# Two transformer blocks on one core: fp32r products in the expert loop, norms and pooling by pairs, modulation in one bank

## The reference

```
first_block, for l in 0, 1:
    h = rms_norm(x);  q, k, v, u, cq, ckv, kpe, gates = split(h @ w_in[l])
    y_a = swa_attention(...)      # window of 128, 8 heads, bias by bucket
    y_b = conformer_conv(u)       # 31 taps, layer norm, silu
    y_c = mla_attention(...)      # 8 heads, dense causal
    x += sum(sigmoid(gates) * ([y_a, y_b, y_c] @ w_branch[l])) @ w_out[l]
    x += square(relu(rms_norm(x) @ w_up[l])) @ w_down[l]
x = rms_norm(x)

second_block, for i in 0, 1:      # ALPHA = 4 ** 0.25
    m = split(silu(c) @ w_mod[i] + b_mod[i], 6)           # 6 x 1024
    y = mixer_retention_na(x * (1 + m[1]) + m[0], ...) if i == 0 else pool_mixer(same)
    x = layer_norm(ALPHA * x + m[2] * y, g, b)
    y = hier_moe(x * (1 + m[4]) + m[3])
    x = layer_norm(ALPHA * x + m[5] * y, g, b)

pool_mixer(h), for group g of 256 features, w = 2, 4, 8, 16:
    z = mean of h over tokens [t - w/2, t + w/2) (clipped to 0..256)  -  h
    out = (z @ pool_w[g]) * pool_scale

hier_moe(t): group = argmax over 4, in it the top 2 of 8 experts, weights by softmax
    acc += (silu(t @ wg) * (t @ wu)) @ wd * weight        # 32 experts, hidden 512
```

## Time and profile before

| | us |
|---|---|
| three runs | 2491.52, 2491.7, 2495.52; median 2491.7 |
| the profiled execution, its own time | 2489.5 |
| its span in the profile | 2487.7 |
| PE busy | 2302.5 (93%) |
| DVE busy | 1003.0 (40%) |
| ACT busy | 457.0 (18%) |
| DMA | 621 MB, 250 GB/s over the span |
| the chain that ended last | PE 85%, DVE 12%, issue 1%, ACT 1%, DMA 1% |

### The profile page before, as it was taken

One profiled execution on the slowest core, in us unless ns is written; L12 is line 12 of the kernel. 1 busy time (PEld: TensorE's weight loads), 2 busy tenths in 40 slices (PEclk: granted clock), 3 DMA queues, 4 the chain that ended last, 5 costly groups with the idle time before them and its releaser, 6 DMA issues.

```text
span 2487.7 us, 31019 instructions
## 1 busy us (share of the span) xinstructions
PE 2302.5 (93%) x12984; PEld 1596.9 (64%) x12984; DVE 1003.0 (40%) x2100; ACT 457.0 (18%) x729; POOL 3.8 (0%) x12
## 2 busy tenths in 40 slices
PE   7998989998999989998997899999995699999996
PEld 6876779997876679997976544444433444444443
DVE  7888535541266335546375311111106511111112
ACT  2112114330123214334242100000000000000000
POOL 0000000000000000000000000000000000000000
PEclk9998999999999999999998899999997899999998
DMA  6435643444435724442213599999974199999991
GB/s 246 165 136 203 248 158 136 169 169 145 160 139 217 288 102 160 178 164 100 99 71 157 213 420 427 427 427 427 428 325 203 60 411 425 425 430 427 426 427 58
DMA packets 43340, 621.45 MB, mean 250 GB/s; under 512 B 4816, under 2 KB 4816, under 8 KB 5232
## 3 DMA queue, kind: packets, MB, share of 16 engines
q1 hardware_dynamic: 33984, 489.93, 48.9%
q10 hardware_dynamic: 8640, 125.83, 11.9%
q0 software_dynamic: 624, 4.39, 0.4%
HBM read 619.08 MB, written 1.05 MB: 249 GB/s over the span
## 4 chain that ended last, share of the span: by engine, by line
PE 85%; DVE 12%; issue 1%; ACT 1%; DMA 1%; DVEq 0%; SPq 0%; ACTq 0%
PE bank L525 24%; PE bank L1087 18%; PE bank L1109 9%; PE sums L1117 5%; PE bank L708 3%; PE bank L709 3%; PE bank L710 3%; PE sums L710 2%; PE sums L709 2%; PE sums L708 2%; DVE wide L1631 2%; PE bank L546 2%; DVE arena L1658 2%; PE bank L535 2%; PE bank L836 2%; PE bank L838 2%
## 5 line engine op out<-in xcount | busy, mean ns | idle before, releaser
L525 PE MATMUL bank<-h,ring 128*128 128x256 f32 x1600 | 359.6, 386 | 15.1 <-DVE h L1556 12.1
L525 PEld LDWEIGHTS bank<-h,ring 128*128 128x128 f32 x1600 | 307.0, 193 | 65.7 <-DVE h L1556 12.9
L1109 PE MATMUL bank<-ring,wide 128*64 128x512 f32 x1024 | 233.8, 598 | 0.0
L1858 DVE TENSOR_TENSOR ring_split<-ring,arena_split 128x2048 fp32r<-128x2048 f32 x64 | 143.8, 2288 | 110.6 <-ACT arena_split L1322 110.4
L2255 DVE TENSOR_TENSOR wide<-bank,wide 128x256 f32<-128x256 f32 x64 | 27.2, 425 | 394.7 <-ACT wide L1485 394.7
L2260 DVE COPY wide<-bank 128x512 f32<-128x512 f32 x64 | 44.3, 692 | 345.1 <-PE bank L1109 345.1
L1485 ACT ACTIVATE wide<-bank 128x256 f32<-128x256 f32 x64 | 24.5, 383 | 751.2 <-PE bank L1087 751.2
L708 PE MATMUL bank<-h_split,arena_split 128*128 128x256 f32 x512 | 146.6, 286 | 15.0 <-DVE ring_split L1858 15.0
L1109 PEld LDWEIGHTS bank<-ring,wide 128*64 128x64 f32 x1024 | 67.8, 136 | 130.8 <-issue 130.8
L525 PE MATMUL bank<-arena,ring 128*128 128x256 f32 x496 | 118.4, 401 | 31.3 <-DVE arena L2301 19.7
L709 PE MATMUL bank<-scratch_split,arena_split 128*128 128x256 f32 x512 | 146.2, 285 | 0.0
(11 more groups left out here) (314 smaller groups left out, 3429.4 us busy)
## 6 DMA issues: line engine op xcount, KB each, us to landing
ring<-in_stream SPq DMA_DIRECT2D x100, 2048.0 KB, 7.8
ring<-in_experts SPq DMA_DIRECT2D x98, 2048.0 KB, 10.0
arena<-in_experts SPq DMA_DIRECT2D x34, 2048.0 KB, 15.2
ring<-in_experts ACTq DMA_DIRECT2D x30, 2048.0 KB, 13.4
arena<-in_experts ACTq DMA_DIRECT2D x30, 2048.0 KB, 13.3
wide<-in_na_bias POOLq DMA_DIRECT2D x1, 1536.0 KB, 9.6
arena<-in_consts POOLq DMA_DIRECT2D x1, 1088.0 KB, 6.4
x<-in_tokens SPq DMA_DIRECT2D x1, 1024.0 KB, 6.0
```

Source lines behind the costliest of these rows:

```text
L525: mm = pe.matmul(dst, a, b, start=(first and i == 0), stop=(i == len(terms) - 1))
L1109: mm = pe.matmul(banks[2][64 * half:64 * half + 64, :], M["turned"][:, e % 2, at:at + 64], w[:, k, 512 * half:512 * half + 512], start=(k ...
L1858: dve.tensor_tensor(split["ring"][:, slot, 2048 * part:2048 * part + 2048], v, HI[("up", "down")[part]][:, j % 2, :].bitcast(F32), ALU.sub ...
```

## The change

Six things at once.

1. **Modulation in one bank a layer.** All 12 chunks of a layer add up in sums[0]. Chunk c takes `cond` shifted by 2c columns, so that its two rows stand at rows 2c and 2c + 1 of each group of 32. One copy on ACT, one turn (`turn_mod`, 4 products of 24 columns) behind the out-projection and one add on DVE follow, in place of 12 of each.
2. **Attended values in sums[1] and sums[3].** `open_attended` uses these two in turn, and not the rotating banks.
3. **fp32r in gather and spread.** Rows of tokens are split in a high part (fp32r, written by ACT) and a low part (`rows_low`, by DVE, difference of bank and high part); the 0/1 matrices are fp32r. A gather is 8 fp32r products in place of 4 of fp32. y is scaled by its slot's weight and split in the same way, the high part by ACT (it waits `down_done` and the weight), the low part by DVE; the turned `weighted` becomes 0/1 by a compare on DVE, and the slot's weight is the sum over its row, by ACT's `accum_out`. A spread is 16 fp32r products of 64 rows in place of 8 of fp32. Gate, up and down stay as they were. The copy of what was turned is cut from 512 to 256 columns.
4. **Norms by pairs of tiles.** Each of the four pairs has its own event, for the residual (`added`), centring (`centred`), squares (now on ACT), scaling by the root (`scaled_by_root`) and h (`h_act`, and `h_dve` for the last pair). Gain, shift and modulation are folded into columns worked out early (`norm_columns`). ACT writes h for tiles 0 to 5 and all of x, DVE h for tiles 6 and 7. The router runs pair by pair, and the output is stored in four DMAs.
5. **Band pooling on PE.** `pool_rows(g)` multiplies h by the pooling weights with tokens on the rows, DVE copies the bank, `pool_band_of(g)` multiplies it by a 256 x 256 band matrix of group g (1 MB in all, loaded by POOL). DVE's box sums go.
6. The prologue's and the loop's memsets of fp32r buffers are products with 0.

```diff
             def mod_site(l, c):
...
+                at = cond_at - 2 * c
+                for k in range(KT):
+                    g = 32 * (k % 4)
+                    mm = pe.matmul(sums[0][g:g + 32, :], cond[:, k, at:at + 32], w[:, k, :], start=(c == 0 and k < 4),
+                                   stop=(c == MOD_CHUNKS - 1 and k >= 4), skip_group_check=True)
+                S.give(mm, "mod_product", l, c)
...
-                if c:
-                    S.wait(pe, "mod_copied", l, c - 1)
-                    if c >= 2:
-                        S.wait(pe, "mod_kept", l, c - 2)
-                    for t in range(4):
-                        mm = pe.matmul(sums[2][:, 2 * t:2 * t + 2], A["mod_rows"][:, (c - 1) % 2, t * P:(t + 1) * P], cst("sum4"),
-                                       start=True, stop=True)
...
+            def open_attended(l, pair):
+
+                b = 1 + 2 * (pair % 2)
+                if pair >= 2:
+                    S.wait(pe, "read", "y", l, pair - 2)
...
                     for a in range(2):
                         k = 2 * j + a
+                        c = (k % 4) * P
                         mm = product(bank[:, a * T:(a + 1) * T],
-                                     [(M["by_token"][:, t, k * P:(k + 1) * P], placed_at[buf][:, t, :]) for t in range(2)])
+                                     [(MS["by_token"][:, t, k * P:(k + 1) * P], place_split[buf][:, t, :]) for t in range(2)]
+                                     + [(rows_low[:, 2 * t + k // 4, c:c + P], place_split[buf][:, t, :]) for t in range(2)])
...
+                    for m in range(4):
+                        for part in (MS["y"], M2S["y_low"]):
+                            for n in (m, m + 4):
+                                a, c = 64 * (n // 4), m * P
+                                pe.matmul(sums[n // 2][:, (n % 2) * T:(n % 2 + 1) * T], part[a:a + 64, c:c + P],
+                                          MS["turned"][a:a + 64, before, T:2 * T], start=False, stop=False, skip_group_check=True)
...
-                        act.activation(M["turned"][:, e % 2, :], banks[1][:, :], ACT.Copy)\
+                        act.activation(M["turned"][:, e % 2, 0:T], banks[1][:, 0:T], ACT.Copy)\
                            .then_inc(S.sem(f"moe{i}_turned"), 1)
+                        act.activation(smax[:, 1, T:2 * T], banks[1][:, T:2 * T], ACT.Copy,
+                                       accum_out=slot_weight[:, e % 2:e % 2 + 1]).then_inc(S.sem(f"moe{i}_weight_summed"), 1)
+                        act.wait_ge(S.sem(f"moe{i}_down_done"), it * 4 + (e + 1))
+                        act.wait_ge(S.sem(f"moe{i}_weight_summed"), it * 4 + (e + 1))
+                        act.activation(MS["y"], banks[2][:, :], ACT.Copy, scale=slot_weight[:, e % 2:e % 2 + 1])\
+                           .then_inc(S.sem(f"moe{i}_y_high"), 1)
...
-                        dve.wait_ge(S.sem(f"moe{i}_down_done"), it * 4 + (e + 1))
-                        dve.tensor_copy(M["y"], banks[2][:, :]).then_inc(S.sem(f"moe{i}_y_kept"), 1)
...
+                        dve.wait_ge(S.sem(f"moe{i}_weight_summed"), it * 4 + (e + 1))
+                        dve.tensor_scalar(MS["turned"][:, e % 2, T:2 * T], banks[1][:, T:2 * T], 0.0, None, ALU.is_gt)\
+                           .then_inc(S.sem(f"moe{i}_slots_turned"), 1)
+                        dve.wait_ge(S.sem(f"moe{i}_y_high"), it * 4 + (e + 1))
+                        dve.scalar_tensor_tensor(out=M2S["y_low"], in0=banks[2][:, :], scalar=slot_weight[:, e % 2:e % 2 + 1],
+                                                 in1=MS["y"].bitcast(F32), op0=ALU.mult, op1=ALU.subtract)\
+                           .then_inc(S.sem(f"moe{i}_y_kept"), 1)
...
+                for b in range(4):
+                    act.wait_ge(S.sem("centred"), S.value("centred", i, s, b))
+                    S.give(act.activation(pair_of(scratch, b), pair_of(x, b), ACT.Square), "post_squares", i, s, b)
+                root(("post", i, s))
...
+                for b in range(3):
+                    act.wait_ge(S.sem("scaled_by_root"), S.value("scaled_by_root", i, s, b))
+                    for k in (2 * b, 2 * b + 1):
...
+                            ins = act.activation(h[:, k, :], x[:, k, :], ACT.Identity, scale=norm_col(i, s, "h_gain", k),
+                                                 bias=norm_col(i, s, "h_shift", k))
+                    S.give(ins, "h_act", i, s, b)
...
+            pe.wait_ge(S.sem("band_landed"), 16)
+            pool_rows(0)
+            pool_rows(1)
+            pool_band_of(0)
+            pool_rows(2)
+            pool_band_of(1)
+            pool_rows(3)
+            pool_band_of(2)
+            pool_band_of(3)
```

More of the change, by code:

```diff
@@ L285, in two_blocks_kernel @@
         scratch = whole["scratch"]
-        wide = sb("wide", [P, 8192])
+        wide = whole["wide"]
         arena = whole["arena"]
@@ L2094, in post_norm @@
                 tag = ("post", i, s)
-                centre(tag, x, KT, D, ("sum", *tag))
+                twice = [P, 2, T]
+                bank = take(dve, "sum", *tag)
+                mean = bank[:, 0:T].unsqueeze(1).to_broadcast(twice)
+                for b in range(4):
+                    v = x[:, 2 * b:2 * b + 2, :]
+                    n = S.give(dve.scalar_tensor_tensor(out=v, in0=mean, scalar=-1.0 / D, in1=v, op0=ALU.mult, op1=ALU.add),
+                               "centred", i, s, b)
@@ L2206, in route @@
                 link(ins)
+                for t, half in ((0, 1), (1, 0), (1, 1)):
+                    keep_low(t, half)
                 bank = take(dve, "rank", i)
```

296 lines of the change are left out of this document (170 added, 126 removed).

## The result

The changed kernel took 2382.5 us (median of four runs, 2380.0 to 2388.1) where the kernel before took 2491.6: a ratio of 0.956, interval 0.954 to 0.958. The prediction was 2385, the range 2358 to 2420. The profiled execution took 2380.0 us with a span of 2378.1, 109.6 less than the 2487.7 of before; the sum of the prediction was 106.6.

The account below looks back on a forecast made before the run. Expert loops were taken as bound by PE and loads at once, layers mostly by PE, seams by DVE and PE alternating. 27 + 20 + 9.2 - 2.6 + 42.8 + 10.2 = 106.6 us off 2489.5, plus 2.2, gave 2385; range 2358 to 2420.

Parts of the forecast that it names:

- Layers: First two layers: modulation in one bank and attended values in their own banks save 27 us, bounds 13 and 34.
- the two DVE waits: Layer 0: DVE's waits of 5.60 and 3.18 us at modulation adds go, together 8.8 us.
- PE's wait with its half-rate stretch: Layer 0: PE's 5.43 us wait for ScalarE's copy of attended values and the half-rate stretch behind go, 5.3 us.
- Loops: Two expert loops: loads become the only bound, each loop ends 9.9 us earlier; 20 us, bounds 8 and 32.
- Entry: Loop entries: faster first gathers save 9.2 us in all, DVE's low parts of rows cost 2.6.
- Norms: Norms, router and output store: work by pairs of tiles saves 42.8 us, bounds 30 and 48.
- Pooling: Band pooling on PE: 25.5 us for 35.7, including a new 2.4 us wait; saves 10.2, bounds 5 and 15.
- A: Rival: expert loops give nothing back, queues alternate and DMA share falls below 1; 2405 us, chance 0.12.
- B: Rival: layers give nothing, DVE or the softmax chain takes up what PE leaves; 2412 us, chance 0.15.
- E: Rival: the load stream speeds up with PE, loops save 103 us instead of 20; 2302 us, chance 0.03.
- C: Rival: seams give more, full clock and no pool wait, 74 us for 59.6; 2370 us, chance 0.12.
- D: Rival: PE pauses in every loop turn, clock falls to half, gain about cancelled or kernel slower; chance 0.03.

Follow-up runs that it names:

- no_spread: Changed kernel without the spread's 16 products an expert inside the loop, all experts but each loop's last missing from the result: 2381.1 us.
- half_loads: Changed kernel with each expert load, except a loop's first six, cut from 2 MB to 1 MB, half of each weight stale: 2308.1 us.
- u_att_mod: Changed kernel with attended values back in the rotating banks and modulation again chunk by chunk: 2412.9 us.
- all_sp: Changed kernel with SP issuing all of an expert's loads, including the middle third that ScalarE issued: 2375.8 us.
- u_loop: Changed kernel with gather and spread back in fp32, one copy of rows and y, no low parts: 2407.0 us.
- u_pairs: Changed kernel with each wait of the four norms for a pair of tiles made a wait for the last pair: 2430.8 us.
- pool_banks: Changed kernel with band products of the third and fourth pooled group in two accumulators of their own, sums 1 and 3: 2378.8 us.
- warm: Changed kernel with unread products added where PE waits, after three norms' sums of squares and ahead of each loop's entry gather: 2377.6 us.

## Why the prediction was right, and where its steps were off

**What bounds the kernel.** Right, and tested in both directions: a shorter turn leaves the loop where it is (no_spread), shorter loads make it 425 us at once (half_loads).

**Layers, 27 predicted, 30.8 measured.** In layer 0 (17.1 for 17) the scores of the last unit come at 248.5 for 263.4, 14.9 us earlier, where the two DVE waits (8.8) and PE's wait with its half-rate stretch (5.3) made 14.1; the rest gave 2.2 for 2.9. The terms are as predicted, not only their sum. That it fits to 0.1 us is luck: three other profiled executions of the same layer ended it 5 us later. Layer 1 is the mis-sized one, 13.8 for 10. PE's waits there for ScalarE's copy of attended values, before and after (us in total, times, longest):

```profile
PE bank L525 <- ACT arena L1186: 3.4, 7, 0.5
```

```profile
PE bank L549 <- ACT arena L1258: 0.8, 1, 0.8
```

There were seven such waits, and I had counted the four on the part of the chain that I had read. The split can be read by setting the starts of the same PE instruction in the two traces against each other, row by row. The lead of the changed kernel grows at each of the eleven sites, not at nine only, by 0.91 us each, the distance from a site's start to the next row's in the kernel before:

```profile
750.68 1.05 PE L777 MATMUL sums<-con,arena 128*128 128x2 f32 x8
751.59 0.53 PE L546 MATMUL bank<-con,smax 128*128 128x128 f32 x3
```

That makes 10.0 for 8.8. The waits for ScalarE's copy give 2.9 for 1.7. A stretch at half clock, which the kernel before had at this place and the changed one did not, gives 1.6 that the sum did not have (windows of the kernel before and, at the same work, the changed one):

```profile
730.00:733.00 3.00, 3.00 (x18) 0.59 (x16) 2.08 (x9) 0.97 (x4) 0.00 (x0) 0.51 0.00 0
712.00:715.00 3.00, 3.00 (x26) 1.35 (x25) 2.76 (x11) 1.29 (x5) 0.00 (x0) 1.00 0.00 0
```

Elsewhere in the layer 0.7 went to the clock, and 13.8 is the sum. The clock's part is of these two executions and no gain to count on: in u_att_mod a further stretch of half clock made layer 1 3.8 us longer than before. The bounds 13 and 34 held.

**Loops, 20 predicted, 18.6 measured.** The landing times were right: the last load lands 447.3 us behind the first product in both loops (449.2 predicted). Window around it in the second loop:

```profile
2335.00:2340.00 5.00, 5.00 (x26) 1.62 (x24) 0.75 (x1) 0.69 (x1) 0.00 (x0) 1.00 0.64 265
```

The fp32r products were a little slower than their nearest rows: gather 1.06 for 0.96, spread 1.14 for 0.96 (0.12 apart, but the first of each block later), a turn 13.2 for 12.9. The other end of the bound, halves that don't overlap, is out. What I had wrong is the pause: not 1.8 us in each turn but 2.49 in every second or third, because two queues carry the loads. all_sp shows it: one queue, one pause of 1.24 a turn. The two loops end 13.6 and 16.2 us behind the last landing, where the sum had 12.5. Most of the difference between them is the clock. In the second loop the last of these pauses stands ahead of the last expert but one, whose gate and up then ran partly at half clock:

```profile
2323.30 8.79 PE L1136 MATMUL bank<-ring,h 128*64 128x512 f32 x32 [2.49 <-DMA ring<-in_experts]
...
2338.24 7.04 PE L1136 MATMUL bank<-arena,h 128*64 128x512 f32 x32
```

That expert took 14.94 us, the one at this place in the first loop 13.24, 1.7 of the 2.6 us by which the two loops differ.

**Entry, 6.6 predicted, 7.5 measured.** The gather gave 4.0 and 4.6 for 4.6 each, the low parts took 0.1 and 1.0 for 1.3 each. u_loop gives back 6.0 of it.

**Norms, 42.8 predicted.** Closing products to centring fell by 4.0 (4.4 predicted), centring to variance is 5.16 (5.3), and the router starts 1.96 us behind the scaling's start (1.9). The last norm with the store gave 11.3 for 12.6: centring and variance gave 4.0 and 4.9 for 4.4 and 4.7, so scaling and store gave 2.4 for 3.5. u_pairs adds what the prediction did not have: how much clock the pairs save, 10.6 us. I had put the pairs down as hidden work alone; where I let the clock fall, at the router, it fell (7.01 us as predicted).

**Pooling, 10.2 predicted.** From the scaling to the next centring 23.7 us for the 25.5 of the working, a gain of 12.0. The wait that was forecast at 2.4 is there with 2.34, and pool_banks takes it away. The half rate was over-sized: the first two groups took 5.1 us where 7.0 had been put.

**The rivals.** A (the loops give nothing) falls by the 18.6 us of u_loop, B (the layers give nothing) by the 30 of u_att_mod, E (the stream speeds up) by no_spread. C was right in its first half only: the seams gave 60.2 for 59.6 and not 74, and the pool wait was there; warm shows that a full clock at the seams has to be paid for with work. D came in part: after 11 of the 18 longer pauses gate and up ran below full clock (8.78 mostly), 1.7 us each, and the 14.68 of the loads hid it but for the last one of the second loop. Had PE been the bound, all of it would have been seen in the time. So one sign that I had named for being wrong, the clock's rows falling inside the loop, did come; the time is right because the loads, and not PE, are the bound there.

The Trainium skill (TensorE: Matmul & The Clock Gate, "Loop structure matters more than you think") had warned of that shape. The trace agrees for pauses of 2.49 us in part of the turns; at 1.83 in every turn (no_spread, 1500 to 1600) and at 1.24 (all_sp) the clock stood at 1.00. The Trainium skill's other place that was weighed (DMA: Bandwidth & Descriptors, "Where 436 GB/s comes from") puts the ceiling at 435 GB/s; the loops stayed at 427 to 429 in the changed kernel, no_spread and all_sp, and ended no 8 us earlier on that account.

## What to carry to other kernels

When a loop stands at two limits at once, work taken from one of them is paid only at the loop's ends; ask how far the last load's landing and the last product are apart, and whether the loads land in the order in which they are used. At a seam between stages, handing over by pairs of tiles was worth more than the sum of the steps that it overlaps, since PE's clock stayed up as well. Before a stage of two profiles is compared to the last us, look at the clock in it: the same instructions ran 5 us longer in another execution. A wait that a change adds is best priced by reading who holds the bank: it can then be named before the run, and taken away after it.

## What the runs showed of the hardware

Loads in flight in two queues share the engines: with the middle third in ScalarE's queue its loads landed 14.1 us after issue and SP's 22.9, and PE waited 2.49 us in every second or third turn; with all in SP's it waited 1.24 each time, at the same 428 GB/s. TensorE's clock fell to 0.50 in the router of warm with PE busy 5.00 of 5 and a wait of only 0.81 us ahead, so a busy engine alone doesn't hold it; what it did there were 32 records of 36 columns. And it stood at 1.00 in a loop where PE waited 1.83 us of each 14.69. The same instructions of layer 0 ran at 1.00 in one execution and at 0.52 in another (118 to 125 us).
